# A top-16 chain moved into PSUM, copies moved to ScalarE, and one low half in sixteen moved from GpSimd to VectorE

## The reference

```python
def peer_ffn(x, w_q, sub_keys, u, v):
    q = (x @ w_q).reshape(B, S, PEER_HEADS, 2, PEER_HALF)        # 8 heads, 2 x 64
    s = jnp.einsum('bshpc,hpnc->bshpn', q, sub_keys)              # 128 keys per half
    s1, i1 = lax.top_k(s[..., 0, :], PEER_TOPK)                   # 16 of 128
    s2, i2 = lax.top_k(s[..., 1, :], PEER_TOPK)
    cand_s = (s1[..., :, None] + s2[..., None, :]).reshape(..., 256)
    cand_i = (i1[..., :, None] * 128 + i2[..., None, :]).reshape(..., 256)
    top_s, pos = lax.top_k(cand_s, PEER_TOPK)                     # 16 of 256
    idx = jnp.take_along_axis(cand_i, pos, axis=-1)
    gate = jax.nn.softmax(top_s, axis=-1)
    hid = jnp.einsum('thkd,td->thk', u[idx], x)
    a = jax.nn.gelu(hid) * gate
    return jnp.einsum('thk,thkd->td', a, v[idx])
```

## Time and profile before

| | before |
|---|---|
| median of 3 runs | 1663.44 us (1662.82 to 1664.09) |
| profiled execution, its own time | 1665.73 us |
| its span | 1664.0 us |
| granted clock of TensorE over the span | 0.994 |
| PE busy | 1625.5 us (98%) |
| DVE busy | 1049.4 us (63%) |
| ACT busy | 975.2 us (59%) |
| POOL busy | 1128.9 us (68%) |

### The profile page before, as it was taken

One profiled execution on the slowest core, in us unless ns is written; L12 is line 12 of the kernel. 1 busy time (PEld: TensorE's weight loads), 2 busy tenths in 40 slices (PEclk: granted clock), 3 DMA queues, 4 the chain that ended last, 5 costly groups with the idle time before them and its releaser, 6 DMA issues.

```text
span 1664.0 us, 30522 instructions
## 1 busy us (share of the span) xinstructions
PE 1625.5 (98%) x10334; PEld 1485.7 (89%) x10334; DVE 1049.4 (63%) x2326; ACT 975.2 (59%) x1962; POOL 1128.9 (68%) x897
## 2 busy tenths in 40 slices
PE   8999999999999999999999999999999999999998
PEld 7888888889998888799998998988999999999997
DVE  2785433334343333755534399996999988889997
ACT  5555665556465555666644667675555566666664
POOL 8445799998989999886645799997899811111120
PEclk9999999999999999999999999999999999999999
DMA  6323455555545555544343465665777788899994
GB/s 233 102 102 114 152 179 188 188 189 167 188 165 190 188 189 189 169 163 138 127 178 101 135 207 192 205 221 192 236 252 252 248 290 287 269 311 313 332 336 157
DMA packets 104318, 334.38 MB, mean 201 GB/s; under 512 B 12144, under 2 KB 26608, under 8 KB 103952
## 3 DMA queue, kind: packets, MB, share of 16 engines
q1 hardware_dynamic: 94368, 294.99, 52.0%
q0 software_dynamic: 9696, 37.91, 7.5%
q10 hardware_dynamic: 144, 0.08, 0.0%
HBM read 324.90 MB, written 7.47 MB: 200 GB/s over the span
## 4 chain that ended last, share of the span: by engine, by line
PE 80%; POOL 9%; issue 4%; DVE 3%; ACT 2%; DMA 1%; SPq 0%; POOLq 0%; DVEq 0%; ACTq 0%
PE bank L776 27%; PE bank L808 16%; PE bank L1437 13%; POOL w_lo L684 8%; PE bank L809 8%; PE bank L1439 6%; PE bank L1414 3%; PE bank L754 1%; PE bank L1326 1%; DMA ring<-stream 1%; ACT w_hi L1493 1%; PE bank L855 1%; PE bank L869 0%; DVE arena L2261 0%; PE bank L1337 0%
## 5 line engine op out<-in xcount | busy, mean ns | idle before, releaser
L684 POOL TENSOR_TENSOR w_lo<-ring,w_hi 128x512 fp32r<-128x512 f32 x804 | 1042.2, 1313 | 243.6 <-ACT w_hi L1493 209.0
L1493 ACT ACTIVATE w_hi<-ring 128x512 fp32r<-128x512 f32 x1060 | 663.2, 630 | 528.2 <-PE bank L809 247.4
L808 PE MATMUL bank<-h_high_and_low,w_hi 128*128 128x448 f32 (+1 forms) x1728 | 583.3, 388 | 4.5 <-POOL w_lo L684 4.5
L809 PE MATMUL bank<-h_high_and_low,w_lo 128*128 128x224 f32 (+1 forms) x1728 | 467.4, 270 | 0.0
L808 PEld LDWEIGHTS bank<-h_high_and_low,w_hi 128*128 128x128 f32 x1728 | 324.9, 188 | 55.1 <-POOL w_lo L684 6.4
L809 PEld LDWEIGHTS bank<-h_high_and_low,w_lo 128*128 128x128 f32 x1728 | 328.7, 190 | 1.6
L1437 PE MATMUL bank<-A_high_and_low,w_hi 128*128 128x448 f32 x1024 | 321.1, 375 | 1.6 <-ACT mask_parts L1963 1.6
L776 PE MATMUL bank<-h_high_and_low,w_hi 128*128 128x256 f32 x1504 | 286.7, 289 | 4.8 <-POOL w_lo L684 4.1
L1439 PE MATMUL bank<-A_high_and_low,w_lo 128*128 128x224 f32 x1024 | 269.3, 263 | 0.0
L776 PEld LDWEIGHTS bank<-h_high_and_low,w_hi 128*128 128x128 f32 x1504 | 241.6, 195 | 8.1 <-issue 3.8
L776 PE MATMUL bank<-h_high_and_low,w_lo 128*128 128x256 f32 x752 | 215.0, 286 | 0.0
(11 more groups left out here) (387 smaller groups left out, 1909.7 us busy)
## 6 DMA issues: line engine op xcount, KB each, us to landing
ring<-stream SPq DMA_DIRECT2D x530, 512.0 KB
spill<-mask_parts SPq DMA_DIRECT2D x56, 112.0 KB
XN<-spill SPq DMA_DIRECT2D x56, 112.0 KB, 5.4
arena<-branch_w POOLq DMA_DIRECT2D x1, 3072.0 KB, 12.6
X<-x SPq DMA_DIRECT2D x2, 512.0 KB, 4.6
arena<-kv_w SPq DMA_DIRECT2D x1, 1024.0 KB, 7.6
out<-X SPq DMA_DIRECT2D x4, 256.0 KB, 2.2
arena<-row POOLq DMA_DIRECT2D x1, 512.0 KB, 5.0
```

The lines of the kernel that those rows point to most:

```text
L684: nc.gpsimd.tensor_tensor(w_lo[:, hs, :], ring[:, slot(phase, e), k * HALF:(k + 1) * HALF], w_hi[:, hs, :].bitcast(F32), ALU.subtract) \
L808: mm(dst[:, 0:2 * n], high, h[:, k, :, 0:n], start=k == 0, stop=False, skip_group_check=True)
L809: last = mm(dst[:, 0:n], low, h_hi[:, k, 0:n], start=False, stop=k == KC - 1, skip_group_check=True)
L1493: A(w_hi[:, half_slot(phase, e, k), :], ring[:, slot(phase, e), k * HALF:(k + 1) * HALF], ACT.Copy).then_inc(rounded, 1)
```

## The change

It has five parts.

1. Banks 0 and 1 become one tensor of 1024 columns. The small chain after the heads puts its intermediate results into PSUM (banks 2 and 3). The selections work on 1024 numbers, four times per tile instead of eight; one sum now stands before each reduce and one after it.
2. The cast of the indices goes from DVE to ACT, at ACT's steps 24 and 58; DVE waits for it (`keys_as_floats`) before the selections.
3. In `peer_early0` the second low half of units 7, 15, 23, 31, 39, 47, 55 and 63 is made by DVE, right after its sum of the unit two before. POOL's loop over 17 turns is written out, and leaves these halves out.
4. SP's load into slot 3 waits for POOL's first halves too, since the two halves of a unit now come from two engines.
5. At the end ACT makes the eight copies out of the banks, and several waits of PE, DVE and SP are replaced by counts of their own.

The diff, cut. The shared names:

```diff
+BY_DVE = range(7, EARLY - 4, 8)
...
-        psum = [ctx.enter_context(nc.psum_tensor(f"bank{b}", [P, 512], F32)) for b in range(8)]
+        banks01 = ctx.enter_context(nc.psum_tensor("banks0_and_1", [P, 1024], F32))
+        psum = [banks01[:, 0:512], banks01[:, 512:1024]]
```

SyncE's queue:

```diff
                             sp.wait_ge(split[slot(p.name, e)], turn_of(p.name, e, i))
+                            if p.name == "peer_early0" and e == 3:
+                                sp.wait_ge(first_split, number(p.name, e, i, 1, 1 - SLOTS))
```

GpSimd:

```diff
-            def split_unit(phase, e, i=0):
-                for k in range(2):
+            def split_unit(phase, e, i=0, halves=range(2)):
+                for k in halves:
...
+                elif p.name == "peer_early0":
+                    for u in range(EARLY - 4):
+                        split_unit(p.name, u % 4, u // 4, range(1 if u in BY_DVE else 2))
```

TensorE, the end:

```diff
-                    pe.wait_ge(*before_turn(second))
+                    pe.wait_ge(ev("by_feature"), 2 * half + 2)
                     mm(bank(second)[:], selector[:], expert_sum[:, cols], start=True, stop=False, skip_group_check=True)
-                    pe.wait_ge(*before_turn(first))
```

ScalarE, in the early stretch and at the end:

```diff
+                    for t, after in enumerate((24, 58)):
+                        if u == after:
+                            act.wait_ge(ev("top_diff"), t + 1)
+                            A(IF[:, t, :, :, :].rearrange("p h k c -> p (h k c)"),
+                              I16[:, t * 256:(t + 1) * 256].bitcast(U32), ACT.Copy).then_inc(ev("keys_as_floats"), 1)
                     for t, after in enumerate((32, 58)):
                         if u == after:
                             act.wait_ge(ev("top_diff"), t + 1)
...
+                for k in range(KC):
+                    act.wait_ge(ev("features_summed"), k + 1)
+                    A(by_feature[:, k, :], bank(f"acc6_{k}")[:, 0:T], ACT.Copy).then_inc(ev("features_copied"), 1)
```

VectorE, in `summed_early` and in the chain after the heads:

```diff
+                        if u + 2 in BY_DVE:
+                            hs = half_slot("peer_early0", (u + 2) % 4, 1)
+                            dve.wait_ge(*half_rounded("peer_early0", (u + 2) % 4, (u + 2) // 4, 1))
+                            V.tensor_tensor(w_lo[:, hs, :], ring[:, slot("peer_early0", (u + 2) % 4), HALF:UNIT],
+                                            w_hi[:, hs, :].bitcast(F32), ALU.subtract) \
+                                .then_inc(split[slot("peer_early0", (u + 2) % 4)], 1)
...
-                    chain(V.tensor_copy(SEL[:, t, 2, 0:PEER_H], TS[:, t, :, 0]))
+                    chain(V.tensor_copy(tops, TS[:, t, :, 0]))
...
-                    chain(V.tensor_copy(IF[:, t, :, :, :].rearrange("p h k c -> p (h k c)"),
-                                        I16[:, half].bitcast(U32)))
-                    chain(V.tensor_scalar(PU2[:, 0, :].bitcast(U32), PU[:, t, :].bitcast(U32), 4, None,
+                    chain(V.tensor_scalar(positions[:, 0, :], PU[:, t, :].bitcast(U32), 4, None,
                                           ALU.logical_shift_right))
...
+                    dve.wait_ge(ev("keys_as_floats"), t + 1)
+                    c4 = chosen.rearrange("p (h c) a -> p h c a", h=4)
                     for k in range(2):
-                        for n in range(4):
...
+                        for n in range(2):
+                            chain(V.tensor_tensor(chosen, places[:, k, 64 * n:64 * n + 64].unsqueeze(2)
+                                                  .broadcast_to([P, 64, 16]),
+                                                  iota16.unsqueeze(1).broadcast_to([P, 64, 16]), ALU.is_equal))
+                            chain(V.tensor_tensor(c4, c4, IF[:, t, 4 * n:4 * n + 4, k, :].unsqueeze(2)
+                                                  .broadcast_to([P, 4, 16, 16]), ALU.mult))
+                            summed_early(1)
+                            chain(V.tensor_reduce(SEL[:, t, k, 64 * n:64 * n + 64], chosen, AX.X, ALU.add))
                             summed_early(1)
```

VectorE, the end:

```diff
-                    V.tensor_copy(by_feature[:, k, :], b[:, 0:T]).then_inc(ev("features_copied"), 1)
                     dve.wait_ge(ev("features_copied"), k + 1)
-                    V.tensor_tensor(by_feature[:, k, :], by_feature[:, k, :], b[:, T:2 * T],
-                                    ALU.add).then_inc(*frees(f"acc6_{k}"))
-                    dve.wait_ge(*read_out(f"acc6_{k}"))
-                    dve.sem_inc(ev("by_feature"), 1)
+                    V.tensor_tensor(by_feature[:, k, :], by_feature[:, k, :], bank(f"acc6_{k}")[:, T:2 * T],
+                                    ALU.add).then_inc(ev("by_feature"), 1)
```

More of the change, by code:

```diff
@@ L296, in build @@
         small = sb("small", [P, NT, NSMALL])
-        psum = [ctx.enter_context(nc.psum_tensor(f"bank{b}", [P, 512], F32)) for b in range(8)]
+        banks01 = ctx.enter_context(nc.psum_tensor("banks0_and_1", [P, 1024], F32))
+        psum = [banks01[:, 0:512], banks01[:, 512:1024]]
+        psum += [ctx.enter_context(nc.psum_tensor(f"bank{b}", [P, 512], F32)) for b in range(2, 8)]
         class Plan:
@@ L598, in _ @@
                             sp.wait_ge(split[slot(p.name, e)], turn_of(p.name, e))
+                        if p.name == "peer_early1" and e == 3:
+                            sp.wait_ge(first_split, number(p.name, e, 0, 1, 1 - SLOTS))
                         sp.dma_start(ring[:, slot(p.name, e), :], stream[p.first + e]) \
```

47 lines of the change are left out of this document (18 added, 29 removed).

## The result

The changed kernel was a little slower: a median of 1666.79 us (1665.45 to 1672.7, 22 runs) against 1663.95 us (1662.06 to 1668.69, 22 runs), a ratio of 1.0017 with a 95% interval of 1.0011 to 1.0024. That is +2.8 us, where -1.9 was predicted, and 1.6 us above the top of the range. By the bound of 0.2% it is "same". On another chip, later, the ratio was 1.0007 (0.9998 to 1.0016).

What follows compares the result with a forecast made beforehand. PE held 80% of the chain, with PE, POOL and DVE within 3% in the heads. Terms -2.0 + 3.3 + 3.3 - 1.0 - 1.8 - 1.1 - 2.6 = -1.9 us gave a 1661.5 us median, range 1657.2 to 1665.2.

Steps and rivals of the forecast that it cites:

- chain after the heads: Small DVE chain between sums 23 and 24: sum 24 comes 2.95 us behind sum 23, unit 28 sooner, -2.0 us.
- halves 31 and 63: DVE's halves behind sums 29 and 61, in the selections: covered by DVE's slack there, cost 0.
- unit 62 behind sum 57: Tile 1's end of heads, where ACT bounds: unit 62 follows 1.0 us earlier, -1.0 us.
- end of the stretch, unit 62 to 68: Sum 67 comes 3.7 us after unit 67's start instead of 5.52, through DVE's slack: -1.8 us.
- the end: Program's end: copies and adds keep PE's pace, DVE's last add ends at 1658.65 instead of 1661.25, -2.6 us.
- The clock: PE's clock at unit 68: idle time shrinks from 4.7 to 2.9 us, clock stays up (0.6 to 0.4), -1.1 us.
- Eight low halves on DVE: Early stretch: 1.1 us per half; six in heads cost +3.3 us in tile 0 and +3.3 in tile 1.
- ACT's step 58: Tile 1, ACT behind sum 57: rounding 4.4 us after it, Gelu 58 at 7.2 us instead of 8.23.
- the places where PE waits for DVE's halves: In the heads, PE waits for DVE's `w_lo` at halves 7, 15, 23, 39, 47, 55, by 0.3 to 1.9 us.
- the halves find the port free: Rival, heads: six halves cost 0.69 us each, half of POOL's 2 us relief arrives; -5.4 us, 1658.0; chance 0.32.
- DVE becomes the bound: Rival, heads: halves wait fully, next candidates lose step, 2.2 us each; +5.8 us, 1669.2; chance 0.08.
- the early stretch cancels out: Rival: early gains equal the halves' cost, leaving the program end's -2.6 us: 1660.8, or 1661.9 with clock down; chance 0.12.

Runs made afterwards that it cites:

- changed_again: The changed kernel unaltered, timed and profiled a second time on another chip: 1666.84 us, ratio 1.0007 to the kernel before.
- cast_on_dve: Changed kernel with no low halves on DVE and the index cast back on DVE: 1659.03 us, ratio 0.9958 to the kernel before.
- exp_later: Changed kernel with ACT's exponentials of tile 1 at step 62 instead of 58: 1665.72 us, ratio 1.0004 to the kernel before.
- no_halves_exp62: Changed kernel with no low halves on DVE and ACT's tile 1 exponentials at step 62: 1658.23 us, ratio 0.9961 to the kernel before.
- halves_only: Kernel before with only parts 3 and 4, the eight low halves on DVE: 1671.07 us, ratio 1.0034 to the kernel before.
- pool_keeps_halves: Changed kernel with all low halves back on POOL: 1658.52 us, ratio 0.9961 to the kernel before.
- sel_halves_exp62: Changed kernel with only halves 31 and 63 on DVE and tile 1's exponentials at step 62: 1659.64 us, ratio 0.9960 to the kernel before.
- chain_alone: Changed kernel with no low halves on DVE and the old end restored: 1660.24 us, ratio 0.9968 to the kernel before.
- same_work_scratch: Changed kernel with POOL making all halves and DVE doing equal, unused subtractions at the same eight places: 1671.20 us, ratio 1.0033 to the kernel before.
- double_halves: Changed kernel with 17 low halves on DVE instead of eight: 1673.33 us, ratio 1.0051 to the kernel before.

## Why the prediction failed, point by point

The middle column is the term of my sum. The last is from the tables; what the clock touches is from changed_again, where it stayed up at unit 61.

| step | predicted | measured |
|---|---|---|
| chain after the heads | -2.0 | -1.9: sum 57 without halves, 149.56 - 151.45 |
| six halves in the heads | +6.6 | +7.8: sum 57, 157.34 - 149.56 |
| halves 31 and 63 | 0 | 0 |
| unit 62 behind sum 57 | -1.0 | -1.15: 9.36 against 10.51 |
| end of the stretch, unit 62 to 68 | -1.8 | -2.0: 19.44 against 21.43 |
| clock at unit 68, unit 68 to 80 | -1.1 | -0.1 and +0.6: 40.83 and 41.51 against 40.93 |
| the end | -2.6 | -2.76: 8.15 against 10.91 |
| sum | -1.9 | -0.1 to +0.6 |

**The step that failed first is "The clock".** It said that the clock would stay up at unit 68, because PE's idle time shrank. The idle time did shrink, from 4.68 us to 2.27 (2.6 in the second execution), and the clock fell all the same, behind the transposes in both executions. That it had stayed up behind waits of 1.5 and 1.3 us was no evidence for one of 2.3. Nor is the length of the wait all that decides: in cast_on_dve the clock stayed up behind a longer one (PE's row, then a window behind it):

```profile
1121.26 0.55 PE L763 MATMUL banks_and<-ident,arena 128*128 128x128 f32 x3 [2.72 <-DVE arena L2745]
1122.00:1124.00 2.00, 1.47 (x10) 1.42 (x11) 0.99 (x3) 0.00 (x0) 0.33 (x1) 1.00 0.00 0
```

And the value of a clock that stays up was misjudged. In exp_later it did stay up, behind waits of 2.33 and 0.73 us. PE's timeline there, from the transposes on (unit 68 starts at 1125.49):

```profile
1123.92 0.55 PE L763 MATMUL banks_and<-ident,arena 128*128 128x128 f32 x3 [2.33 <-DVE arena L2749]
1125.19 0.55 PE L763 MATMUL banks_and<-ident,arena 128*128 128x128 f32 x3 [0.73 <-DVE arena L2749]
...
1137.50 0.44 PE L817 MATMUL bank<-h_high_and_low,w_hi 128*128 128x448 f32 x1 [0.84 <-POOL w_lo L690]
1146.22 0.44 PE L817 MATMUL bank<-h_high_and_low,w_hi 128*128 128x448 f32 x1 [1.68 <-POOL w_lo L690]
```

Unit 80 nevertheless came 41.12 us behind unit 68, no sooner than the 40.93 of before. PE, faster at first, waits 2.5 us for POOL's low halves there, where the kernel before waited once, 1.56 us. In cast_on_dve and no_halves_exp62, where the clock stayed up too, it was 41.13. After the transposes PE waits for POOL, and what the clock gives back is waited away. So against the kernel before the term was 0, and not -1.1, even where the clock stayed up. That does not make the clock worth nothing: in the kernels where it was low for some 7 us from about unit 68 on (halves_only, pool_keeps_halves, sel_halves_exp62), unit 80 came 42.1 to 42.2 us behind unit 68.

**The second is the size of "Eight low halves on DVE".** The instruction itself was right: the six in the heads last 1.62 + 0.75 + 0.68 + 1.67 + 1.10 + 0.76 = 6.58 us, and 6.6 was predicted. What I left to a rival, that the next candidates are thrown out of step, happened once in each tile (1.51 and 1.50 us instead of about 0.55). The candidates took 11.6 us instead of 9.8, and 1.2 us of that arrive at sum 57. That rival had the mechanism, but not the price, 1.3 a half instead of 2.2.

**Right** were the chain (2.89 us, 2.95 predicted), ACT's step 58 (4.38 and 7.06, predicted 4.4 and 7.2), the places where PE waits for DVE's halves, and the end. The end of the stretch was right in its number, and partly by luck: sum 67 came 3.71 us behind the start of unit 67, where 3.7 was predicted, but chain_alone has the same slack on DVE and it came 5.44 behind, because of the load that the prediction did not look at. The rival "the halves find the port free" is refuted: its price was 0.69 a half, and its relief of 2 us did not appear beside it. So is "the early stretch cancels out": at unit 80 the changed kernel was 3.3 to 3.4 us behind the kernel before. The weights were wrong too: I gave that case 0.32, and the case in which DVE becomes the bound 0.08.

The rule of the Trainium skill, "SBUF — State Buffer", section "Who interferes with whom", says that the first comer keeps the shared port for its whole instruction; the prediction's estimate from it was a mean wait of half of POOL's 1.30 us. With POOL relieved of nothing (same_work_scratch) the mean wait of eight was 0.70, so the trace agrees. With POOL relieved it was 0.31. By that estimate's 8.0 us for six halves sum 57 would have been right to 0.2, though in part for another reason, the candidates.

**What stays open.** These terms give at most +0.6 us, the medians +2.8 and +1.3. From unit 0 to the end of the span the two profiled executions of the changed kernel took 2.4 and 0.6 us more than that of the kernel before, and the terms with the fall near 1331 us (1.6 to 1.7, in the first alone) account for both. So what is left of the medians, and why the two measurements differ, must lie ahead of unit 0, whose start varies from 940.5 to 945.5 us over the profiles, or in how often the clock falls, and only one execution of a run shows its falls. No run settles it.

## What to carry to other kernels

Work moved from a full engine to another full engine has to be priced in the order of the engine that takes it, with the instructions behind it: a half that cost nothing in the selections cost 1.3 us in the heads.
```profile
1012.39 1.19 DVE L2701 TENSOR_SCALAR arena<-arena 128x128 uint32<-128x128 uint32 x1
```

- GpSimd got longer beside VectorE as well: from 951 to 1005 us none of its halves took more than 1.50 us in the kernel before, and the two that ran against DVE's halves of units 7 and 15 in the changed kernel took 1.74 and 1.73.
- MAX8 and FIND_INDEX8, SBUF to SBUF, did not get longer: over 256 numbers their means were 0.43 and 0.42 us with and without the halves.
- The wait repeats from kernel to kernel, as if set by the phase of the two engines: the half of unit 7 (or the instruction in its place) took 1.62 us in the changed kernel, in halves_only, in double_halves and in same_work_scratch.
- The clock's fall is not a fixed property of a kernel. Behind the same 1.58 us wait for ACT's `mask_parts` near 1331 us it fell in three of 14 profiled executions, and in the changed kernel in one of two. The fall at unit 61 cost 1.1 us at first: from the start of unit 61 to that of unit 67 it was 16.75 us with it and 15.60 without. But at unit 80 the two executions were 0.04 us apart, so it was waited away.
